# A two-layer encoder trunk on one core: the GpSimd split of 1024 weight columns in the mixer written as two operations of 512 columns

## What is computed

```python
for l in range(DEPTH):
    h = rms_norm(x, mix_norm_g[l])
    proj = h @ w_in[l]                      # 1024 x 4096: eight groups of 512 columns
    da_q, da_k, da_v, hg_q, hg_zf, hg_zb, hg_i, hg_g = split_cols(proj, IN_SIZES)
    y_a = diff_attention(...)               # 4 heads, softmax1 - lambda * softmax2
    y_b = hgrn2_bidirectional(...)          # 4 heads, gated recurrence in both directions
    x = x + jnp.concatenate([y_a, y_b.astype(y_a.dtype)], axis=-1) @ w_out[l]
    x = x + conv_glu_ffn(rms_norm(x, ffn_norm_g[l]), w_up[l], conv_w[l], conv_b[l], w_down[l])
```

## Time and profile before

| | us |
|---|---|
| median of 3 executions | 1376.87 (1375.77 to 1378.2) |
| the profiled execution, its whole time | 1376.25 |
| its span, first to last instruction | 1374.5 |
| PE busy in it | 1346.1 |
| POOL busy | 709.3 |
| DVE busy | 918.4 |

### The profile page before, as it was taken

How to read it: one execution, slowest core, us unless ns; L and a number is a source line. 1 busy time by engine, 2 the same in 40 slices (tenths; PEclk the granted TensorE clock), 3 DMA queues, 4 the chain that set the end, 5 groups by cost and what they waited for, 6 DMA issues and landing times.

```text
span 1374.5 us, 20262 instructions
## 1 busy us (share of the span) xinstructions
PE 1346.1 (98%) x7650; PEld 1091.3 (79%) x7650; DVE 918.4 (67%) x1078; ACT 628.6 (46%) x912; POOL 709.3 (52%) x539
## 2 busy tenths in 40 slices
PE   9999999999999999999999999999999999999999
PEld 6778777877888888888877777777778888888887
DVE  7687899555888888600356789986558888885001
ACT  6353666574444444321444536665644444443121
POOL 2795565246444444444568935752474444444443
PEclk9999999999999999999999999999999999999999
DMA  5233122123333333333332322221223333333333
GB/s 189 78 92 86 49 69 77 47 62 92 96 104 92 94 106 93 93 106 94 92 92 77 93 70 64 61 70 47 77 91 94 98 101 92 96 104 93 92 105 108
DMA packets 37139, 121.50 MB, mean 88 GB/s; under 512 B 4928, under 2 KB 5440, under 8 KB 37056
## 3 DMA queue, kind: packets, MB, share of 16 engines
q1 hardware_dynamic: 36768, 119.84, 29.5%
q10 hardware_dynamic: 288, 0.52, 0.1%
HBM read 114.05 MB, written 2.10 MB: 85 GB/s over the span
## 4 chain that ended last, share of the span: by engine, by line
PE 72%; DVE 13%; POOL 5%; issue 5%; ACT 4%; DMA 0%; DVEq 0%; ACTq 0%; POOLq 0%
PE bank L566 22%; PE bank L568 22%; PE bank L567 22%; DVE QQ L1424 2%; POOL KK L531 2%; POOL wL L504 1%; DVE A L1403 1%; DVE sm L1461 1%; POOL wL L498 1%; DVE E L1469 1%; PE bank L717 1%; DVE sqR L1351 1%; DVE hL L406 1%; DVE tmp L1328 1%; DVE swp L1330 1%
## 5 line engine op out<-in xcount | busy, mean ns | idle before, releaser
L504 POOL TENSOR_TENSOR wL<-raw,wH 128x1024 fp32r<-128x1024 f32 x142 | 342.9, 2415 | 404.5 <-ACT wH L902 294.3
L566 PE MATMUL bank<-hH,wH 128*128 128x512 f32 x1216 | 484.3, 398 | 8.7 <-POOL wL L498 6.1
L568 PE MATMUL bank<-hL,wH 128*128 128x512 f32 x1216 | 475.0, 391 | 0.0
L567 PE MATMUL bank<-hH,wL 128*128 128x512 f32 x1216 | 474.3, 390 | 0.0
L498 POOL TENSOR_TENSOR wL<-raw,wH 128x256 fp32r<-128x256 f32 x268 | 240.4, 927 | 188.0 <-ACT wH L902 188.0
L566 PEld LDWEIGHTS bank<-hH,wH 128*128 128x128 f32 x1216 | 228.9, 188 | 73.0 <-issue 16.0
L568 PEld LDWEIGHTS bank<-hL,wH 128*128 128x128 f32 x1216 | 228.7, 188 | 49.3
L567 PEld LDWEIGHTS bank<-hH,wL 128*128 128x128 f32 x1216 | 229.2, 188 | 45.6 <-issue 0.5
L902 ACT ACTIVATE wH<-raw 128x1024 fp32r<-128x1024 f32 x173 | 182.6, 1056 | 157.1 <-PE bank L568 156.8
L1576 DVE TENSOR_TENSOR x<-x,bank 128x512 f32<-128x512 f32 x16 | 10.9, 683 | 200.7 <-PE bank L568 200.7
L566 PE MATMUL bank<-gH,wH 128*128 (+1 forms) x352 | 137.2, 390 | 0.0
(11 more groups left out here) (175 smaller groups left out, 1735.7 us busy)
## 6 DMA issues: line engine op xcount, KB each, us to landing
raw<-wts SPq DMA_DIRECT2D x210, 512.0 KB, 3.6
x<-xT SPq DMA_DIRECT2D x8, 256.0 KB, 5.7
swp<-K SPq DMA_DIRECT2D x32, 64.0 KB, 2.0
swp<-QO SPq DMA_DIRECT2D x32, 64.0 KB, 2.4
outT<-x SPq DMA_DIRECT2D x8, 256.0 KB, 2.0
raw<-wts ACTq DMA_DIRECT2D x2, 256.0 KB, 4.6
raw<-wts SPq DMA_DIRECT2D x2, 256.0 KB, 5.8
W<-pos SPq DMA_DIRECT2D x1, 256.0 KB, 5.4
```

The costliest lines, as they stand in the source:

```text
L504: pool.tensor_tensor(wL[:, s, :], raw[:, s, :], wH[:, s, :].bitcast(F32), ALU.subtract)\
L566: pe.matmul(out, wH[:, s, a:a + P], rhs_h, start=first, stop=False)
L567: pe.matmul(out, wL[:, s, a:a + P], rhs_h, start=False, stop=False)
L568: return pe.matmul(out, wH[:, s, a:a + P], rhs_l, start=False, stop=last)
```

## The change

`split(u)` makes two operations of 512 columns in place of four of 256. The columns, the operands and the result are the same, and the signal `w_split` still comes after the last of them. `split_whole` and all other engines' code stay as they were.

```diff
                         s = u % 2
                         pool.wait_ge(*w_high.at(l, u + 1))
-                        for q in range(4):
-                            at = slice(q * UNIT // 4, (q + 1) * UNIT // 4)
+                        for q in range(2):
+                            at = slice(q * UNIT // 2, (q + 1) * UNIT // 2)
                             m = pool.tensor_tensor(wL[:, s, at], raw[:, s, at], wH[:, s, at].bitcast(F32), ALU.subtract)
                         m.then_inc(w_split.sem, 1)
```

## The result

The changed kernel is slower: median 1384.54 us of 5 executions (1384.18 to 1387.72), beside 1377.39 us of before (5 executions); the ratio is 1.0062, with a 95% interval from 1.0051 to 1.0073. That is +7.1 us in the medians. Its profiled execution took 1387.72 us, 3.2 us above its own median.

The account below looks back on a forecast made before the run. PE was taken to bound the kernel, busy 1346.1 of 1374.5 us. Terms -1.3 + 2.4 + 0.6 + 0.5 = +2.2 us gave 1378.45 for the profiled execution, 1379.1 for the median, taken as 1379.0; 8-in-10 range 1375.5 to 1383.

Parts of the forecast that it names:

- the first rival: Every `W` and `K` meeting a first half on the saturated stretch delays PE by 0.54 us: +5.4, 1382 us; chance 0.2.
- a draw: DVE's burst before PE's wait for `QO`: four waits of 0.55 us become two of 1.09, 2.2 either way, nothing lost.
- The operations: POOL's mixer splits: 2 x 1.27 = 2.54 us each, 0.27 less than 2.81; over 67 splits 18 us of POOL's time.
- The levels: First levels of each layer, where PE waits for POOL's split: PE about 0.7 us earlier, 0.6 in layer 1; gain 1.3.
- their second half: Layer 1's forget gates ahead of PE's wait at 811.63: one extra wait of 0.54 us, loss 0.5, bounds 0 and 0.8.
- The saturated stretch: From 151 to 226 us, and likewise in layer 1, DVE has no idle time: loss 1.2 us a layer, 2.4 together.
- The three `W` and the `K`: Behind the `QO` wait, these four DVE operations each meet a first piece: 4 x 0.54 = 2.2 us, part taken back.
- `E` at 186.52: DVE's `E` takes 1.30 us instead of 0.49, waiting for `KK`; a DVE 0.5 us late waits 0.5 less there.
- more than half meet a split: Of the 32 `W` operations before the change, median 1092 ns, minimum 750; each that meets one costs DVE 0.54 us more.
- Late in the layer: PE's 1.21 us wait for `W` until 288.14: `W` ends some 0.75 later; loss 0.3 a layer, 0.6 together.

## Why the prediction was wrong

The forecast was 1379.0 us, a small loss; the measured time is 1384.54, outside of the range to 1383.0 and beyond the first rival's 1382. The idea was right: DVE waits for the length of the piece that it meets. The step that failed is the list of places where this reaches PE. The burst ahead of `QO` was put at nothing as "a draw" and cost 0.5 us a layer. The sixth level of layer 0 (1.2 us) and the first half of layer 1's forget gates (some 1.7) had no term. Nor had the clock, which cost 3.5 us or more in the profiled execution. By the prediction's steps:

**The operations.** Right: 1266 ns for the half, and the shortest split takes 2.50 us after 2.79, 0.29 less with 0.27 forecast. But POOL's busy time fell by 39 us and not 18. The rest is time inside the operations above their undisturbed length, 57 us before and 35 now: fewer pieces meet fewer of DVE's operations.

**The levels.** Right: 0.7 us in layer 0, and in layer 1 the delay falls from 6.1 to 5.5 us over them. The run with halves there alone gave 1.1 us in PE's starts of the profiles, with 1.3 forecast.

**"For a long burst this is a draw."** This step was nearly right for the burst and wrong for what surrounds it. In the changed kernel the four operations and PE's wait behind them read:

```profile
156.76 3.48 DVE L1424 TENSOR_TENSOR QQ<-QQ,T 128x512 f32<-128x512 f32 x2
160.28 1.29 DVE L1433 TENSOR_TENSOR T<-T 128x512 f32<-128x512 f32 x2
...
163.06 1.03 DVE L1332 TENSOR_TENSOR QO<-tmp,swp 128x512 f32<-128x512 f32 x1
```

QQ and T take 3.48 + 1.29 us where they took 2.38 + 2.25 (rows 7): 0.14 us more, nearly a draw. But the burst comes with other things that the sum left out. `QO` of line 1332 takes 1.03 us, where it took 0.69. It begins at 163.06, 0.13 us after POOL's operation on the factors `T` at 162.93; before, it began at 162.37, just ahead of the one at 162.40. PE's wait for `QO` is 2.34 after 1.83, 0.5 us a layer, forecast as nothing.

**What was not seen at all.** Two stretches in which PE had not waited for DVE before have no term in the sum. The first is the sixth level of the first pair in layer 0. The timeline of DVE before:

```profile
93.26 2.40 DVE L1424 TENSOR_TENSOR QQ<-QQ,T 128x512 f32<-128x512 f32 x2
95.58 1.23 DVE L1351 TENSOR_TENSOR sqR<-sq,sqR 128x512 fp32r<-128x512 f32 x1
```

and in the changed kernel, with PE's start behind it:

```profile
93.24 2.97 DVE L1424 TENSOR_TENSOR QQ<-QQ,T 128x512 f32<-128x512 f32 x2
96.13 1.77 DVE L1351 TENSOR_TENSOR sqR<-sq,sqR 128x512 fp32r<-128x512 f32 x1
...
98.00 0.48 PE L616 MATMUL bank<-sqR,meanR 128*128 128x512 f32 x1 [0.90 <-issue]
```

`QQ` and `sqR` together end 1.1 us later (97.90), and PE stands idle for 0.90 us up to the matmul on `sqR` at 98.00; the row names no releaser, but `sqR` had just ended. So the lead of 0.7 us from the levels has become a delay of 0.5 at 110. The second is the forget gates of layer 1. The prediction priced only their second half, ahead of 811 us; the first half, ahead of 735 us, ended just in time for PE before, and now has PE waiting 1.51 us; the run with halves only there shows it alone. For the second half the forecast was 0.5 us; PE's delay grows from 5.5 us behind the levels to 6.2 at 817.85, by 0.7. A look at how early DVE's results came would have pointed at both places, as it was done for `W` at 189. Before, line 1392's `QQ` ended 0.3 us ahead of PE's start on it, and `sqR` 0.95 us ahead (96.81 and 97.76), of which the lead won at the levels alone uses 0.8: a PE that comes earlier has less cover.

**Why such chains lose more than a draw.** The prediction took a meeting with a quarter to cost 0.55 us and with a half 1.09. For the operations of a chain, each of which starts only when the one before has signalled, the rows give other numbers. Line 1378 (duration in ns) before

```profile
L1378 DVE TENSOR_SCALAR T<-T x8: 426/427/847, 712.2 to 805.4; 128x512 f32<-128x512 f32 x8
```

and in the changed kernel:

```profile
L1378 DVE TENSOR_SCALAR T<-T x8: 427/914/1541, 716.0 to 811.6; 128x512 f32<-128x512 f32 x8
```

Undisturbed it takes 427 ns, behind a quarter at most 847, behind a half up to 1541: waits of 0.42 and 1.11 us, and for `W` 0.35 and 0.92. My reading, which no run tests, is that part of a piece passes in the pause between two such operations, and of a half hardly more passes there than of a quarter. By these largest waits, four quarters cost 4 x 0.42 = 1.7 us and two halves 2 x 1.11 = 2.2. That each split costs DVE half a microsecond more wherever a chain runs beside it is an estimate from these rows.

**The saturated stretch** from 165 to 228 us: the delay grew by 1.45 us in layer 0 and by 1.5 in layer 1, forecast 1.2. The three `W` and the `K` hold: each takes 0.55 us longer. Something like 0.8 of these 2.2 us is taken back, but not at `E`, where the prediction put it. `E` at 186.52 took 1.30 us (rows 8) and still does; the operation on `sm` just ahead of it gives 0.25. It took 0.77 us before, and in the changed kernel the rows are

```profile
187.00 0.52 DVE L1468 TENSOR_TENSOR sm<-sm,lamc 128x1 f32<-128x1 f32 x1
187.55 1.30 DVE L1469 TENSOR_SCALAR E<-E,sm 128x512 f32<-128x512 f32 x1
188.88 1.67 DVE L1472 SCALAR_TENSOR_TENSOR W<-E,sm 128x512 f32<-128x512 f32 x1
```

The same operation gives 0.57 us ahead of `E` at 165.85 (1.03 before, 0.46 now), where the prediction saw no delay to make good: DVE was already 1.0 us late. The forecast that `W`'s median would rise to 1.6 us was wrong, although those `W` that meet a piece do take 1.64 to 1.67 us: with halves, 14 of 32 meet one and 18 don't (late in a layer `sm` and `E` meet it instead). 17 of 32 did before: "more than half meet a split" was true, by one.

**Late in the layer.** `W`'s result comes 0.77 us later (PE's idle 1.98 after 1.21), as forecast 0.75. In the run with halves only late and no loss of clock there, PE's starts at 290.94 and 318.57 are 27.63 us apart, where they were 28.15 before: 0.5 of it is made good, a net loss of 0.25, the forecast 0.3. In the changed kernel's profiled execution they are 28.93 apart, 1.3 us more, and that is the clock.

**The clock** had no term in the sum at all. Three stretches at the lower level are new in the profiled execution, behind idle times of 1.7 to 2.0 us of PE (near 291, 817 and 981 us). Its mean clock is 0.994 and it took 1387.72 us; the execution with 0.998 took 1384.18. By this comparison of two executions the three cost about 3.5 us together. PE's starts put them higher: from 817.85 to 855.63 the delay grows by 2.1 us, 0.5 of it the wait for `QO`, which leaves some 1.5 for that stretch alone. Either way about 7 to 8 of the 11.3 us between the profiles are there without them. On the page the 11.3 us are 5.7 of busy time of PE (1351.8 after 1346.1) and 5.6 of idle time, for a stretch at the lower clock counts as busy. The other executions lie in between, at 0.995 to 0.997. So longer waits can cost twice, once themselves and once in what follows, and the second part varies from execution to execution. The kernel before varies in the same way: 1375.38 to 1375.68 us in three executions of one chip at a mean clock of 1.000, and 1378.08 and 1378.16 in two at 0.996. What exactly makes the clock fall in one execution and not in another with the same waits stays open; no run was made on it. Nor is the mean clock of an execution a price by itself: with whole splits, one execution with 0.944 took 1399.38 us and one with 0.994 took 1399.30.

Of the rivals, the first had the right sign and came nearest in size, but not by its own working. It wanted the 2.2 us of the three `W` and the `K` to reach PE in full; PE's delay grew by 1.45 and 1.5 there, near the forecast's 1.2. About half of what the loss exceeds the forecast by came from the stretches that were not priced. That the Trainium skill's rule ("SBUF — State Buffer", section "SBUF: two separate sides", a lock held for the whole instruction) decides here is borne out by the pair with the long piece first and last, and by `W`'s 1115, 1673 and 2764 ns.

## What to carry to other kernels

Where GpSimd and VectorE work on SBUF side by side, the length of a GpSimd operation is a latency that VectorE pays each time it meets one; size it by which of the two engines the critical engine waits for at that place, short where VectorE is behind, long where GpSimd is, and put the short pieces first. Before calling a stretch covered because nobody waits in it, read how much earlier than needed the result comes there: two places with 0.3 and 0.95 us to spare made over a third of this loss. And beside an edit's effect on idle times of TensorE, reckon with what they do to its clock: that costs time where TensorE is what bounds, and little where it would wait for VectorE anyway.

## What the runs showed of the hardware

- The wait of a VectorE operation behind a GpSimd one grows with the GpSimd operation's length, within 10 ns between these sizes: `W`'s longest duration is 1115, 1673 and 2764 ns for pieces of 256, 512 and 1024 columns (715, 1266 and 2359 ns long undisturbed).
- A GpSimd TENSOR_TENSOR of two float32 operands took at least 448, 715, 1266 and 2359 ns for 128, 256, 512 and 1024 columns: about 2.1 ns a column and 0.17 us for the operation.
- Idle times of TensorE of only 1.7 to 2.3 us were followed by a fall of its granted clock (from 2.4 to 1.2 GHz) in some executions; behind those of 1.4 us at the levels it stayed at 1.00, and behind the 1.74 us at 811.63 of the kernel before too. Behind the wait for `QO` near 164 us it fell in the kernel before (1.83 us, 0.61 in the stretch from 164 to 168) and stayed at 1.00 with the long piece last (1.84 us).
- A fall of the clock near 817 us cost some 1.5 us. The one near 165 us cost some 0.2: with halves only at layer 1's gates it does not occur, and TensorE was 1.5 us ahead near 168 us but 0.2 at 185.49, having waited 0.47 us for `W` and 0.98 for `ev`.
